# Tail sums over 96 stacked partitions, an earlier zero fill and moved last-step tables in a one-core decoder layer

## The reference

```
x1 = layer_norm(ALPHA * x + (1 + gt1) * mix, ln1_g, ln1_b)
h  = x1 * (1 + sc2) + sh2
z  = silu(h @ w_gate[e]) * (h @ w_up[e]) * weight        # for its two experts e
f  = sum over the two experts of z @ w_down[e]
x  = layer_norm(ALPHA * x1 + (1 + gt2) * f, ln2_g, ln2_b)
```

## Time and profile before

| | us |
|---|---|
| median of 3 runs | 622.52 (622.03 to 624.54) |
| profiled execution, its own time | 623.2 |
| span of that execution | 621.4 |
| PE busy | 492.7 (79%) |
| DVE busy | 225.2 (36%) |
| ACT busy | 156.7 (25%) |
| POOL busy | 114.5 (18%) |
| DMA, hardware queue of SP | 150.74 MB, 62.2% of 16 engines |

### The profile page before, as it was taken

How to read it: one execution, slowest core, us unless ns; L and a number is a source line. 1 busy time by engine, 2 the same in 40 slices (tenths; PEclk the granted TensorE clock), 3 DMA queues, 4 the chain that set the end, 5 groups by cost and what they waited for, 6 DMA issues and landing times.

```text
span 621.4 us, 8713 instructions
## 1 busy us (share of the span) xinstructions
PE 492.7 (79%) x2920; PEld 264.1 (43%) x2921; DVE 225.2 (36%) x572; ACT 156.7 (25%) x339; POOL 114.5 (18%) x175
## 2 busy tenths in 40 slices
PE   1869999999987999984345776448887988788994
PEld 0448787788633344432331332113433344333442
DVE  0342543142686259899670111010111021111144
ACT  1211434532756203222001111010122121111233
POOL 5030002000084440011010121120222222222200
PEclk9969999999999799988557799688999899999998
DMA  8994864420492951215999599999999898999822
GB/s 276 399 349 184 283 239 162 177 73 0 186 373 57 410 129 68 88 50 218 366 420 330 220 414 420 419 421 419 420 400 408 348 419 320 410 416 362 306 89 85
DMA packets 48544, 172.99 MB, mean 278 GB/s; under 512 B 14776, under 2 KB 24048, under 8 KB 33134
## 3 DMA queue, kind: packets, MB, share of 16 engines
q1 hardware_dynamic: 39034, 150.74, 62.2%
q0 software_dynamic: 9136, 21.76, 9.6%
q10 hardware_dynamic: 340, 0.09, 0.1%
HBM read 162.07 MB, written 27.71 MB: 305 GB/s over the span
## 4 chain that ended last, share of the span: by engine, by line
PE 61%; DMA 17%; DVE 11%; issue 6%; ACT 2%; SPq 2%; POOL 0%; POOLq 0%; DVEq 0%; ACTq 0%
PE PB L1658 17%; PE PB L1933 15%; DMA wB<-in_w_up 9%; PE PB L1958 7%; PE PB L1828 6%; DMA ada_m<-in_w_ada 4%; PE PB L1595 2%; PE PB L1982 2%; DMA ada<-in_w_ada 2%; PE PB L1727 1%; PE PB L1797 1%; PE PB L1912 1%; PE PB L1756 1%; PE PB L1670 1%; PE PB L1980 1%
## 5 line engine op out<-in xcount | busy, mean ns | idle before, releaser
L1933 PE MATMUL PB<-wA,XT 128*32 128x512 f32 x480 | 115.0, 633 | 43.8 <-DMA wB<-in_w_up 23.8
L1933 PE MATMUL PB<-wB,XT 128*32 128x512 f32 x480 | 114.9, 634 | 0.0
L1658 PE MATMUL PB<-hT,win 128*128 128x256 f32 (+1 forms) x448 | 103.9, 392 | 2.0 <-DVE hT L1066 2.0
L1658 PEld LDWEIGHTS PB<-hT,win 128*128 128x128 f32 x448 | 86.0, 194 | 22.5 <-issue 9.4
L1933 PEld LDWEIGHTS PB<-wA,XT 128*32 128x32 f32 x480 | 37.3, 116 | 115.0 <-issue 110.4
L1958 PE MATMUL PB<-wA,zT 128*32 128x512 f32 x240 | 55.8, 606 | 5.7 <-ACT zT L946 5.7
L1504 DVE SCALAR_TENSOR_TENSOR z<-silu_g,w_now,PB 128x256 f32<-128x256 f32 x15 | 7.2, 481 | 145.8 <-ACT silu_g L944 145.8
L1958 PE MATMUL PB<-wB,zT 128*32 128x512 f32 x240 | 55.8, 608 | 0.0
L1828 PE MATMUL PB<-wout,yT 128*128 128x512 f32 x112 | 48.8, 593 | 0.0
L944 ACT ACTIVATE silu_g<-PB 128x256 f32<-128x256 f32 x15 | 5.7, 383 | 135.1 <-PE PB L1933 135.1
L1510 DVE TENSOR_TENSOR yo<-PB,gate_row 128x512 f32<-128x512 f32 x15 | 10.4, 692 | 70.7 <-PE PB L1958 65.7
(11 more groups left out here) (427 smaller groups left out, 686.0 us busy)
## 6 DMA issues: line engine op xcount, KB each, us to landing
wB<-in_w_gate SPq DMA_DIRECT2D x24, 1024.0 KB, 15.5
wB<-in_w_up SPq DMA_DIRECT2D x24, 1024.0 KB, 19.6
wB<-in_w_down SPq DMA_DIRECT2D x24, 1024.0 KB
ada<-in_w_ada POOLq DMA_DIRECT2D x12, 1024.0 KB, 7.5
ada<-in_w_ada SPq DMA_DIRECT2D x8, 1024.0 KB, 11.9
wA<-in_w_gate SPq DMA_DIRECT2D x8, 1024.0 KB, 15.4
wA<-in_w_up SPq DMA_DIRECT2D x8, 1024.0 KB, 18.6
wA<-in_w_down SPq DMA_DIRECT2D x8, 1024.0 KB
```

The costliest lines, as they stand in the source:

```text
L1658: last = pe.matmul(B[(q % 2) * 2 + h][:, 0:cn], win[:, n % 3, k, col:col + P], hT[:, k, c0:c0 + cn], start=(k == 0), stop=(k == KD - 1))
L1933: last = pe.matmul(B[2][32 * g:32 * g + 32, :], XT[:, k, 32 * g:32 * g + 32], gu[:, :, k, :], start=(k == 0), stop=(k == KD - 1))
```

## The change

1. The tail's add_up takes x1 and both experts' rows stacked over 96 partitions: each 32 tokens are a group, and a matmul of 96 rows by 32 columns (`stack`, ones on two blocks and ALPHA on the third) sums them. Four such matmuls, one per column group, make a half tile; they replace three of 128 by 128. POOL makes `stack`. y_dram's rows are laid out in groups of 32 tokens, choice by choice, so that one load brings 64 partitions; x1 comes by 32. The loads become eight for x1 and eight for y, and land in other buffers.
2. The zero fill's eight stores follow the h2 store of i = 3 (the sample tile) instead of standing ahead of i = 4.
3. The last-step tables move behind VectorE's first copy of transposed rows, with four operations more for the new row layout; wl's copy and its wait move behind steps_ready; TensorE's first transposes no longer wait for steps_ready.
4. The 25 small loads for the sample rows move behind the loop of weight loads.

```
...
+SG = 32
+YROWS = 2 * T + 2 * SG
...
-        yy = [row(f"yy{t}", [P, 2, D], "r", 8192 * t) for t in range(TT - 1)] + [row(f"yy{TT - 1}", [P, 2, D], "h", 0)]
+        parts = [row(f"parts{t}", [P, TT, D], "x", 16384 * t) for t in range(TT - 1)] + [row(f"parts{TT - 1}", [P, TT, D], "r", 0)]
...
             for i, t, n in MIX:
-                if i == TT:
+                sp.wait_ge(h2_ready, i + 1)
+                sp.dma_start(h_dram[t * P:t * P + n, :], h2[0:n, i % 2, :]).then_inc(h2_stored[i % 2], 16)
+                if i == TT - 1:
                     sp.wait_ge(rows_ready, 3)
                     for c in range(2):
                         for b in range(TT):
-                            sp.dma_start(y_dram[c * NT + b * P:c * NT + (b + 1) * P, :], X[0][:, :]).then_inc(x1_stored, 16)
-                sp.wait_ge(h2_ready, i + 1)
-                sp.dma_start(h_dram[t * P:t * P + n, :], h2[0:n, i % 2, :]).then_inc(h2_stored[i % 2], 16)
+                            sp.dma_start(y_dram[(c * TT + b) * P:(c * TT + b + 1) * P, :], X[0][:, :]).then_inc(x1_stored, 16)
                 sp.wait_ge(x1_ready, i + 1)
...
             sp.dma_start(ln2b[:, :], A["ln2_b"].broadcast_to((P, D))).then_inc(lnp_in, 16)
-            sp.dma_start(sam[:, 0, :], x1_dram[T:NT, :].rearrange("r (q d) -> (r q) d", d=SD)).then_inc(lnp_in, 16)
-            for r in range(NS):
-                sp.dma_start(sam[PS * r:PS * (r + 1), 1, :], m_dram[r, 5, :].rearrange("(q d) -> q d", d=SD)).then_inc(lnp_in, 16)
-            for n, a in ((2, "ln2_g"), (3, "ln2_b")):
...
+            sp.dma_start(sam[:, 0, :], x1_dram[T:NT, :].rearrange("r (q d) -> (r q) d", d=SD)).then_inc(lnp_in, 16)
...
             earlier_out = sp.value_load(earlier_i[0:1, 0:1], min_val=32 * (MINSTEP - 1), max_val=32 * MAXSTEP)
...
-            sp.dma_start(x_tok[:, 0:TT, :], x1_dram[0:T, :].rearrange("(t p) d -> p t d", p=P)).then_inc(yy_in[TT], 16)
+            for t in range(TT):
+                x1 = x1_dram[t * P:(t + 1) * P, :].rearrange("(a h p) d -> h p a d", h=2, p=SG)
+                for h, at_ in ((0, 2 * SG), (1, 0)):
+                    sp.dma_start(parts[t][at_:at_ + SG, h::2, :], x1[h]).then_inc(yy_in[TT], 16)
             sp.wait_ge(y_out, earlier_out)
             for t in range(TT):
-                sp.dma_start(yy[t][:, :, :], y_dram.rearrange("(c n) d -> n c d", c=2)[t * P:(t + 1) * P, :, :]).then_inc(yy_in[t], 16)
+                y_ = y_dram[2 * t * P:2 * (t + 1) * P, :].rearrange("(a h q) d -> h q a d", h=2, q=2 * SG)
+                for h in range(2):
+                    sp.dma_start(parts[t][SG * h:SG * (h + 2), h::2, :], y_[h]).then_inc(yy_in[t], 16)
...
             pool.memset(X[0][:, :], 0.0).then_inc(rows_ready, 1)
+            for h, b in ((0, 0), (1, 1)):
+                link(pool.tensor_tensor(stack[:, h, :], ident[:, b * SG:(b + 1) * SG], ident[:, (b + 1) * SG:(b + 2) * SG], ALU.add))
+                link(pool.tensor_scalar(per_row[:, 0:SG], ident[:, 2 * (1 - b) * SG:(2 * (1 - b) + 1) * SG], ALPHA, None, ALU.mult))
+                link(pool.tensor_tensor(stack[:, h, :], stack[:, h, :], per_row[:, 0:SG], ALU.add))
...
-            dve.wait_ge(place_ps, 2)
-            dve.tensor_copy(wl[:, :], B[3][:, 64:64 + NSTEP]).then_inc(idx_made, 1)
...
             dve.memset(st1[:, 3:4], 0.0).then_inc(y_v, 1)
+            dve.wait_ge(place_ps, 2)
+            dve.tensor_copy(wl[:, :], B[3][:, 64:64 + NSTEP]).then_inc(idx_made, 1)
...
             copy_XT(0)
+            link(dve.tensor_scalar(last_step_f[:, :], steps_f[:, :], -1.0, None, ALU.add))
...
+            step(dve.tensor_scalar(of_choice[:, :], idx_all[:, 1, :], NT - 0.5, float(SG), ALU.is_gt, ALU.mult))
+            step(dve.tensor_scalar(group_i[:, :], idx_all[:, 0, :], 5, None, ALU.arith_shift_right))
...
+            link(dve.tensor_tensor(of_choice[:, :], of_choice[:, :], idx_all[:, 0, :], ALU.add))
+            link(dve.scalar_tensor_tensor(out=idx_all[:, 1, :], in0=group_i[:, :], scalar=float(SG), in1=of_choice[:, :],
+                                          op0=ALU.mult, op1=ALU.add))
...
             one(0, True)
...
-            pe.wait_ge(steps_ready, 1)
             pe.wait_ge(X_in[0], 16)
             transpose_X(0, 0)
             transpose_X(0, 1)
+            pe.wait_ge(steps_ready, 1)
...
             def add_up(t):
-                bank = PB[PAIR[t]]
-                pe.wait_ge(yy_in[t], 32)
+                pe.wait_ge(yy_in[t], 48)
                 for c in range(2):
-                    half = slice(c * 512, (c + 1) * 512)
-                    pe.matmul(bank[:, c, :], aident[:, :], x_tok[:, t, half], start=True, stop=False)
-                    for e in range(2):
-                        pe.matmul(bank[:, c, :], ident[:, :], yy[t][:, e, half], start=False, stop=False)
+                    for g in range(TT):
+                        pe.matmul(PB[PAIR[t]][SG * g:SG * (g + 1), c, :], stack[0:3 * SG, g % 2, :], parts[t][0:3 * SG, g, c * 512:(c + 1) * 512],
+                                  start=True, stop=False)
```

More of the change, by code:

```diff
@@ L195, in build @@
         per_row = row("per_row", [P, P], "w", 19456)
-        aident = row("aident", [P, P], "w", 19968)
+        stack = row("stack", [P, 2, SG], "w", 19968)
         sam = row("sam", [P, 4, SD], "w", 20480)
@@ L206, in build @@
         no_sample = row("no_sample", [P, NSTEP], "w", 23040)
+        of_choice = row("of_choice", [P, NSTEP], "w", 23488)
+        group_i = row("group_i", [P, NSTEP], "w", 23680, I32)
         earlier_i = row("earlier_i", [P, 1], "w", 23424, I32)
@@ L534, in _ @@
                             later_expert(e + q, wB[b][:, q, :], (False, True), dB_in[b])
+            sp.dma_start(sam[:, 0, :], x1_dram[T:NT, :].rearrange("r (q d) -> (r q) d", d=SD)).then_inc(lnp_in, 16)
+            for r in range(NS):
+                sp.dma_start(sam[PS * r:PS * (r + 1), 1, :], m_dram[r, 5, :].rearrange("(q d) -> q d", d=SD)).then_inc(lnp_in, 16)
+            for n, a in ((2, "ln2_g"), (3, "ln2_b")):
+                for r in range(NS):
+                    sp.dma_start(sam[PS * r:PS * (r + 1), n, :], A[a][0].rearrange("(q d) -> q d", d=SD)).then_inc(lnp_in, 16)
             earlier_out = sp.value_load(earlier_i[0:1, 0:1], min_val=32 * (MINSTEP - 1), max_val=32 * MAXSTEP)
@@ L1515, in _ @@
             copy_XT(0)
+            link(dve.tensor_scalar(last_step_f[:, :], steps_f[:, :], -1.0, None, ALU.add))
+            step(dve.tensor_scalar(earlier_i[:, :], last_step_f[:, :], 32.0, None, ALU.mult))
+            step(dve.tensor_scalar(is_last[:, :], sgrid[:, :], last_step_f[:, 0:1], float(NOWHERE), ALU.is_equal, ALU.mult))
+            step(dve.scalar_tensor_tensor(out=of_last[:, :], in0=sgrid[:, :], scalar=last_step_f[:, 0:1], in1=idx_all[:, 0, :],
+                                          op0=ALU.is_equal, op1=ALU.mult))
+            step(dve.tensor_scalar(of_choice[:, :], idx_all[:, 1, :], NT - 0.5, float(SG), ALU.is_gt, ALU.mult))
+            step(dve.tensor_scalar(group_i[:, :], idx_all[:, 0, :], 5, None, ALU.arith_shift_right))
+            step(dve.tensor_scalar(no_sample[:, :], idx_all[:, 0, :], T - 0.5, float(NOWHERE), ALU.is_gt, ALU.mult))
+            step(dve.tensor_scalar(no_prompt[:, :], idx_all[:, 0, :], T - 0.5, float(NOWHERE), ALU.is_lt, ALU.mult))
+            settle()
+            link(dve.tensor_tensor(of_choice[:, :], of_choice[:, :], idx_all[:, 0, :], ALU.add))
+            link(dve.scalar_tensor_tensor(out=idx_all[:, 1, :], in0=group_i[:, :], scalar=float(SG), in1=of_choice[:, :],
+                                          op0=ALU.mult, op1=ALU.add))
+            step(dve.tensor_tensor(idx_all[:, 2, :], idx_all[:, 1, :], no_prompt[:, :], ALU.add))
+            link(dve.tensor_tensor(no_sample[:, :], no_sample[:, :], is_last[:, :], ALU.add))
+            step(dve.tensor_tensor(idx_all[:, 1, :], idx_all[:, 1, :], no_sample[:, :], ALU.add))
+            link(dve.tensor_reduce(tok_last[:, 0:1], of_last[:, :], AX.X, ALU.add))
+            for b in range(1, TT):
+                step(dve.tensor_scalar(tok_last[:, b:b + 1], tok_last[:, 0:1], float(-b * P), None, ALU.add))
+            settle()
+            for b in range(TT):
+                step(dve.tensor_scalar(tok_hot[:, b * P:(b + 1) * P], lanes_f[:, :], tok_last[:, b:b + 1], None, ALU.is_equal))
             one(0, True)
```

11 lines of the change are left out of this document (5 added, 6 removed).

## The result

The changed kernel takes 615.63 us, median of 4 runs (613.87 to 616.45); beside it the kernel before took 622.46. The ratio is 0.988, 95% interval 0.985 to 0.991: 7 us faster, where 17 were forecast, and outside the forecast range. The profiled execution took 616.45 us, its span is 614.7.

What follows compares the result with a forecast made beforehand. Bound: a chain of the expert stage's serial start, weight loads, TensorE's steps and tail sums. Start 3.7 + 1.5 = 5.2 and tail 12.0 give 17.2 less than 623.2: 606.0, or 605.5 against the runs; range 600 to 612.5.

Steps and rivals of the forecast that it cites:

- I take 0.7 us off the gain: Tail loads: allowance for each writing 64 or 32 partitions instead of 128, reducing the tail's gain from 12.7 to 12.0 us.
- The upper bound of 6.2: Tail row loads: if half the partitions bring half the rate, TensorE ends at 605.5, 6.2 us later.
- No cost: 25 small loads behind the loop: SP issues x1 at 569.9 (before: 569.57), and x1 lands by 583.
- Rival (d): SP's small loads hold back the tail beyond 0.72 us per issue; at 2.0 each the time is 638; chance 0.03.
- first sum at 15.6 behind E and 14.2 us of sums: Tail: TensorE starts at 585.1, four tiles of 3.54 us; E is the end of the last-but-one step's down matmuls.
- 12.0 gained: Tail: shorter sums bring VectorE's end from 618.04 to 605.3, 12.7 us, less 0.7 for the loads.
- the 3.7 of the sum: Start of the expert stage: first transposes, freed from the step-table signal, begin at 321.0, a gain of 3.7 us.
- The bound of 2.4: Start: least gain, with both gathers landing at about 322.3, at latest 10.4 and 8.8 us after issue.
- the direct gain is nothing: Zero filling moved ahead: weights done by about 322 instead of 331, but the first step did not wait for them.
- (a): Rival: loads bind the tail at half rate, end 5.5 us later than forecast, 611; chance 0.10.
- (b): Rival: the start does not come forward; gain only 12.0 to 14.4 us, time 608.5 to 610.5; chance 0.09.
- (c): Rival: column groups in the tail sums don't overlap; tail +6.9 us, start -5.2, time 624; chance 0.03.

Runs made afterwards that it cites:

- e2: Kernel before plus only the new tail sums with their layout and 32- and 64-partition loads; fill, tables and small loads at their old places: ratio 0.992.
- e3: Changed kernel with the sample's 25 small loads ahead of the expert loop again: 610.1 us, ratio 0.979.
- e8: As e7, but the same bytes in narrow loads: x1 in four of 32 partitions, the rows in eight of 64: 624.4 us, ratio 1.001.
- e1: Changed kernel with the old tail (x1, rows and sums as in the kernel before), small loads still behind the loop: 621.0 us, ratio 0.995.
- e4: Changed kernel with every tail load writing 128 partitions and x1 summed by its own product: 615.6 us, ratio 0.987.
- e10: As e4 (128-partition tail loads), with the small loads ahead of the loop as in e3: 609.7 us, ratio 0.979.
- e5: Changed kernel with the sample's 25 small loads made into 4 loads of the same packets, at the same place: 610.4 us, ratio 0.979.
- e11: Kernel before with only the zero filling moved: 619.7 us, ratio 0.994.
- e6: Changed kernel with the 25 small loads inside the loop, ahead of the last down weights: 616.8 us, ratio 0.990.
- e9: As e3, but x1 always on partitions 0 to 31 and each tile's rows in one load on 32 to 95: 610.0 us, ratio 0.979.
- e7: Kernel before with only fill and tables moved; old tail sums, x1 in four loads of 128 partitions: 614.3 us, ratio 0.985.

## Why the prediction was wrong

**The step that failed: the loads of the tail.** "I take 0.7 us off the gain, near the lower end, since three quarters of the partitions are written in all." The sum over all loads decided nothing; each load by itself writes one half of the partitions, or, for every second row load, a part of both, and moves 223 to 248 GB/s in all where wide loads move 409. The upper bound of 6.2 had that rate for the rows, and the Trainium skill's page "SBUF — State Buffer" was quoted for it. What the bound left out is x1: its loads have the same form, were checked only against their own deadline ("lands by 583"), and run in the rings together with the scatter that the row loads wait for. e2 and e3 show 3 us for that, e8 5.6 (scatter lands − E).

**The second: "No cost" for the 25 small loads.** All of its working held for SP: 0.46 us each, x1 issued ahead of need. The cost lies in the rings, behind the issue: 6.5 us (e3), 7.3 (e1), 6.3 (e4 against e10), none with four loads (e5). How they cost it in the rings is not shown. Rival (d) had the right edit and the wrong place, SP's issue time.

**The third: TensorE's clock in the tail.** The sum took matmul durations at full clock from a TensorE that came straight from the last step. With 10.96 us of idle time ahead, the first tile took 7.0 us instead of 3.8.

The account of the tail, against the forecast's first sum at 15.6 behind E and 14.2 us of sums: first sum 10.2 later; first tile at the lower clock 3.3; a wait for the third tile's rows 1.1; the pace, 3.77 us per tile instead of 3.54 (a round of add_last takes 1.91 us beside the column groups, not 1.73), 0.9. That is 15.5; the 0.7 allowed for loads and some 0.3 of VectorE's lag were in the forecast already: 14.5, the distance between 12.0 gained and 2.5 lost.

**The start came out better than forecast (7.5 us for 5.2), in part for another reason.** The transposes waited for the gather, as forecast, and came 4.0 us earlier by the place matmuls (2.9 by the store) for the 3.7 of the sum. The bound of 2.4 had the landings the wrong way round: the first transposes need only the first gather, and it was the one that took 8.8 us before, landing at 320.7; the second took 10.4. After the change the first took 8.71, so it did not land sooner. The gap shrank by 4.3 us, not 1.5, of which the slower gate/up (9.59 for 8.60) took 1.0 back. It was put down to the small loads; e11 shows that the filling closes it with them still in place. Against "the direct gain is nothing" for the fill, the fill gained 3.4 us. VectorE's moved block was hidden: it ends at 325.5, and the first product waits for ScalarE until 334.9.

**Rivals.** (a) loads that bind the tail was the right one for the rows, with a chance of 0.10 and without the price of x1; the small loads, the other cause, were (d)'s edit. (b) and (c) are refuted by the transposes and by 1.92 us for sixteen records.

**Open.** Between the row loads' issue and the first sum lie 6.6 to 6.8 us in e2, e3 and e5, but 9.5 in the changed kernel and 10.8 in e6, the two with narrow loads and 25 small ones behind the first step; the records don't say which packets wait there. Whether the last step's scatter, which falls into that stretch, is the one was not tried.

## What to carry to other kernels

Before a layout that saves matmuls is chosen, look at which partitions each single load writes: one that stays in 0 to 63 or in 64 to 127 halves the rate of the rings (224 GB/s for 409 here) for everything that shares them, above all for a store that a later step waits for. Count loads, not only bytes, where they stand in the rings ahead of something that is waited for: a load that costs nothing to issue can still delay what is queued behind it. And bound a change by the transfer that it delays, not only by the transfer's own deadline.

## What the hardware showed that was not expected

64 partitions are written at 398 GB/s when they lie across the middle (32 to 95) and at about half of that inside one half. Whether loads that alternate between the halves overlap is not shown: x1's 2 MB landed 14.1 us behind the first issue in e3 (eight loads, alternately on 64 to 95 and 0 to 31), 15.3 in e9 (four loads, all on 0 to 31), 17.1 in e8 (four loads, quarter by quarter from below) and 10.6 in e7 (128 partitions), each from the first issue to the last one plus the longest landing time, beside other traffic that differs too. 21 loads of 4 KB more, without more data, cost 7.5 us of tail. The gap behind the first gate/up, in which an instruction packet stands, was 6.47 us with the DMA engines 84% busy (338.0 to 344.4 us), mostly on small packets at its start, and 2.11 with them 22% busy (e11, 339.6 to 341.7); that the packet is its cause remains inferred.
